# A decoder step on Trainium2: gathering the first expert's tokens channel-major from rounded high and low parts

## What is computed

```python
def moe_swiglu(h, w_router, b_router, we_gate, we_up, we_down):
    logits = (h @ w_router).astype(jnp.float32) + b_router.astype(jnp.float32)
    top_val, top_idx = lax.top_k(logits, TOP_K)          # TOP_K = 2 of 8
    gates = jax.nn.softmax(top_val, axis=-1)
    combine = jnp.sum(jax.nn.one_hot(top_idx, N_EXPERTS, dtype=jnp.float32) * gates[..., None], axis=-2)
    out = jnp.zeros_like(h)
    for e in range(N_EXPERTS):
        out = out + combine[..., e:e + 1] * swiglu(h, we_gate[e], we_up[e], we_down[e])
    return out
```

## Time and profile before

| | |
|---|---|
| median of three runs | 1937.91 us |
| profiled execution | 1939.48 us |
| its span | 1937.6 us |
| PE busy | 1819.5 us, 94% of the span |
| PE weight loads | 1424.8 us, 74% |
| DVE busy | 1270.0 us, 66% |
| ACT busy | 1065.4 us, 55% |
| POOL busy | 174.6 us, 9% |
| HBM read / written | 480.46 / 17.35 MB |

### The profile page before, as it was taken

One profiled execution on the slowest core, in us unless ns is written; L12 is line 12 of the kernel. 1 busy time (PEld: TensorE's weight loads), 2 busy tenths in 40 slices (PEclk: granted clock), 3 DMA queues, 4 the chain that ended last, 5 costly groups with the idle time before them and its releaser, 6 DMA issues.

```text
span 1937.6 us, 23755 instructions
## 1 busy us (share of the span) xinstructions
PE 1819.5 (94%) x8733; PEld 1424.8 (74%) x8733; DVE 1270.0 (66%) x1223; ACT 1065.4 (55%) x1054; POOL 174.6 (9%) x169
## 2 busy tenths in 40 slices
PE   7988988999998977988799999999999999999997
PEld 6776444899997955435488888888888888888884
DVE  5543133534436874123499898988889988889895
ACT  5433123332315357313387778778787787877672
POOL 4220010000002940010100000000000000000010
PEclk9989999999998988999799999999999999999999
DMA  9451316544435532416399999999999999999993
GB/s 308 157 160 56 120 66 227 181 145 134 147 123 180 196 126 83 138 52 201 134 378 384 368 391 366 386 381 366 392 368 391 379 374 390 364 397 369 385 384 132
DMA packets 236754, 497.88 MB, mean 257 GB/s; under 512 B 15010, under 2 KB 46899, under 8 KB 236670
## 3 DMA queue, kind: packets, MB, share of 16 engines
q1 hardware_dynamic: 223645, 479.11, 68.6%
q0 software_dynamic: 4544, 13.57, 1.9%
q10 hardware_dynamic: 8496, 4.33, 0.8%
HBM read 480.46 MB, written 17.35 MB: 257 GB/s over the span
## 4 chain that ended last, share of the span: by engine, by line
PE 53%; DMA 2%; DVE 2%; ACT 1%; issue 0%; POOL 0%; DVEq 0%; SPq 0%; ACTq 0%; POOLq 0%
PE bank L1150 45%; PE bank L547 4%; DMA big<-in_we_down 1%; PE bank L1209 1%; DMA small_ring<-in_we_down 1%; PE bank L1170 1%; PE bank L1122 0%; DVE big_r L2966 0%; PE bank L1160 0%; PE bank L1187 0%; PE bank L642 0%; ACT big_r L1728 0%; ACT small_ring_r L1728 0%; PE bank L913 0%; PE bank L934 0%
## 5 line engine op out<-in xcount | busy, mean ns | idle before, releaser
L1728 ACT ACTIVATE big_r<-small_ring 128x2048 fp32r<-128x2048 f32 x240 | 456.6, 1916 | 141.8 <-DMA small_ring<-in_we_up 49.0
L2966 DVE TENSOR_TENSOR small_ring_r<-small_ring,big_r 128x2048 fp32r<-128x2048 f32 x192 | 437.2, 2288 | 38.0 <-ACT big_r L1728 37.1
L1150 PE MATMUL bank<-big_r,hT_r 128*128 128x512 f32 x1024 | 384.1, 393 | 1.6 <-DVE kM_r L2972 1.6
L1150 PE MATMUL bank<-small_ring_r,hT_r 128*128 128x512 f32 x768 | 301.0, 392 | 0.0
L1150 PE MATMUL bank<-big_r,kM_r 128*128 128x512 f32 x704 | 274.2, 390 | 0.0
L2966 DVE TENSOR_TENSOR big_r<-big,small_ring_r 128x2048 fp32r<-128x2048 f32 x96 | 219.4, 2290 | 35.6 <-ACT small_ring_r L1728 35.4
L1150 PEld LDWEIGHTS bank<-big_r,hT_r 128*128 128x128 f32 x1024 | 192.3, 188 | 41.2 <-issue 1.8
L1728 ACT ACTIVATE small_ring_r<-big 128x2048 fp32r<-128x2048 f32 x96 | 183.5, 1916 | 50.4 <-DMA big<-in_we_up 27.5
L1150 PEld LDWEIGHTS bank<-small_ring_r,hT_r 128*128 128x128 f32 x768 | 144.2, 188 | 29.8
L1150 PEld LDWEIGHTS bank<-big_r,kM_r 128*128 128x128 f32 x704 | 132.3, 188 | 26.6
L1728 ACT ACTIVATE big_r<-big 128x2048 fp32r<-128x2048 f32 x59 | 113.2, 1919 | 44.4 <-DMA big<-in_we_up 12.8
(11 more groups left out here) (400 smaller groups left out, 2898.2 us busy)
## 6 DMA issues: line engine op xcount, KB each, us to landing
small_ring<-in_we_gate SPq DMA_DIRECT2D x80, 1024.0 KB, 6.3
small_ring<-in_we_up SPq DMA_DIRECT2D x64, 1024.0 KB, 6.1
big<-in_we_down SPq DMA_DIRECT2D x64, 1024.0 KB, 6.2
big<-in_we_up SPq DMA_DIRECT2D x48, 1024.0 KB, 7.0
small_ring<-in_we_down SPq DMA_DIRECT2D x48, 1024.0 KB, 6.2
big<-in_we_gate SPq DMA_DIRECT2D x32, 1024.0 KB, 5.5
small_ring<-in_w_gate SPq DMA_DIRECT2D x11, 1024.0 KB, 5.4
small_ring<-in_w_up SPq DMA_DIRECT2D x11, 1024.0 KB, 7.9
```

The source lines that it names most:

```text
L1150: ins = mm(dst, x_hi_lo[xa][kk], wcols, start=(m < 2 or j == 0) and kk == 0 and (xa, wa) == (0, 0), stop=(m < 2 or j == STAGES - 1) and kk ...
L1728: return A(out, in_, ACT.Copy)
L2966: V.tensor_tensor(low[i % PRING], raw[i % PRING], high[i % PRING].bitcast(F32), ALU.subtract) \
```

## The change

Expert 0's rows are no longer gathered as rows and transposed. ACT rounds `h` to high parts `rows_hi` (three copies of up to 128 x 1024), behind the transposed copies of `h`. DVE writes the low parts `rows_lo`: two ahead of the wait for the logits, the third ahead of the wait for the ranks. The selection is written in fp32r (`first_P`). PE then multiplies parts of `h` as the stationary operand by the selection as the moving one, so that the result is channel-major: for each of 8 channel groups and 3 row tiles one product of 128 columns, 24 for the high parts into banks 7 and 6 and 24 for the low parts into banks 5 and 4. ACT copies the high banks to `moe_x[0]`, DVE the low banks to `moe_x[1]`. Step 2 and the transposes are gone. Rounds after the first (which this input doesn't reach) keep the old way.

```diff
+        first_P = hT_r[:, 1024:1408].rearrange("p (t c) -> p t c", t=3)
+        rows_hi = [qz_r[:, 0:D], qz_r[:, D:2 * D], rounded("vM")[:, :]]
+        rows_lo = [kN_r[:, 0:D], v_r[:, 0:D], Pr_r[:, :]]
...
-            def gather(n, r=None):
+            def gather_first():
+
+                pe.wait_ge(*at("x_hi", "rows", 2))
+                pe.wait_ge(moe_sel, 1)
+                for part, (rows, top, done) in enumerate(((rows_hi, 7, moe_picked), (rows_lo, 5, moe_gathered))):
+                    for half in range(2):
+                        for k in range(4):
+                            c0 = (4 * half + k) * P
+                            for t in range(TILES):
+                                ins = mm(bank[top - half][:, k * P:(k + 1) * P], rows[t][0:ROWS[t], c0:c0 + P],
+                                         first_P[0:ROWS[t], t, :], start=t == 0, stop=t == TILES - 1)
+                        ins.then_inc(done, 1)
+
+            def gather(r):
...
             def expert_round(r):
                 rr = None if type(r) is int else r
-                gather(r * NE, rr)
+                if rr is None:
+                    gather_first()
+                    pe.wait_ge(moe_xhi, 2)
+                else:
+                    gather(r)
...
             norm_squares(5)
             to_hT(5, range(TILES))
+            for t in range(TILES):
+                act.wait_ge(*at("h", 5, t))
+                copy(rows_hi[t][0:ROWS[t]], h[0:ROWS[t], t, :]).then_inc(*sets("x_hi", "rows", t))
             act.wait_ge(*at("choice", "gap"))
...
                 weights_hi(r * NE, 0)
-                rows_out(r)
-                tokens_hi(r * NE)
+                if type(r) is int:
+                    for half in range(2):
+                        act.wait_ge(moe_picked, half + 1)
+                        copy(moe_x[0][:, 4 * half:4 * half + 4, :],
+                             bank[7 - half][:, :].rearrange("p (k c) -> p k c", k=4)).then_inc(moe_xhi, 1)
+                else:
+                    rows_out(r)
+                    tokens_hi(r * NE)
...
+            def rows_low(t):
+                dve.wait_ge(*at("x_hi", "rows", t))
+                V.tensor_tensor(rows_lo[t][0:ROWS[t]], h[0:ROWS[t], t, :], rows_hi[t][0:ROWS[t]].bitcast(F32), ALU.subtract)
+
+            dve.wait_ge(*at("v_out", 1))
+            rows_low(0)
+            rows_low(1)
             b = take("rt")
...
             step(V.tensor_tensor(gates, lg, m8, ALU.add))
+            rows_low(2)
             b = take("rank")
...
-                tokens_lo(r * NE)
+                if type(r) is int:
+                    for half in range(2):
+                        dve.wait_ge(*primed(moe_gathered, half + 1))
+                        V.tensor_copy(moe_x[1][:, 4 * half:4 * half + 4, :],
+                                      bank[5 - half][:, :].rearrange("p (k c) -> p k c", k=4)).then_inc(moe_xT, 1)
+                else:
+                    tokens_lo(r * NE)
```

More of the change, by code:

```diff
@@ L1161, in scatter @@
                    moe_y[:, hf * HALF:(hf + 1) * HALF], start=True, stop=True).then_inc(done, 1)
-            def gather(n, r=None):
-                pe.wait_ge(moe_sel, 1 if r is None else r + 1)
-                if r is not None:
-                    pe.wait_ge(moe_addedE, r * 6)
+            def gather_first():
[10 more added lines that the diff above has]
+            def gather(r):
+                pe.wait_ge(moe_sel, r + 1)
+                pe.wait_ge(moe_addedE, r * 6)
                 for half in range(2):
@@ L1173, in gather @@
                 for half in range(2):
-                    pe.wait_ge(moe_rows_at_hand, (half + 1) if r is None else r * 2 + (half + 1))
+                    pe.wait_ge(moe_rows_at_hand, r * 2 + half - 1)
                     for k in range(4):
@@ L2914, in select_first @@
                     dve.wait_ge(*primed(moe_gathered, r * 2 * NE))
+                chosen = first_P if type(r) is int else moe_P
                 for t in range(TILES):
                     rows = ROWS[t]
-                    ins = V.tensor_scalar(moe_P[0:rows, t, :], C("iota")[0:rows], posr[0:rows, t, 0:1], None, ALU.is_equal)
+                    ins = V.tensor_scalar(chosen[0:rows, t, :], C("iota")[0:rows], posr[0:rows, t, 0:1], None, ALU.is_equal)
                 ins.then_inc(moe_sel, 1)
```

## The result

Over 20 executions of each, the kernel before has a median of 1935.2 us and the changed one 1941.05 us. The ratio is 1.0035, with a 95% interval of 1.0025 to 1.0045: 5 to 9 us slower. The forecast was 1939 us with a range of 1933.5 to 1944.5, which holds the time. But it was 1.1 us above the median known then (1937.9, three runs), and the measured difference is 5.9 us by the medians and 6.8 by the ratio, just past the 0.3% that was set as the bound. Two executions far off the rest, 2097 us of the kernel before and 3676 us of f2, are left out of the ratios.

A forecast was written before the change was run, and what follows sets the result against it. PE was taken to set the pace from expert 0's first product on. Products 0, wait behind the gather -1.9 and clock +2.1 gave +0.2 us (1938.1 beside the median); a +1.0 correction made 1939 us, range 1933.5 to 1944.5.

The forecast's parts named there:

- likeliest case: The forecast's main case for the whole kernel: its own range 1936 to 1943 us, chance 0.64.
- What bounds the kernel: Expert stage, some 960 us: PE sets the pace from expert 0's first product, so shifting its start shifts the end.
- The products of the gather: Gather on PE: 48 products at a weight-load floor of 0.215 take 10.3 us, old gather 10.4; term 0.
- Behind the gather: From gather's end to expert 0's first product: 2.9 us becomes 1.0, gain 1.9 us, bounds 1.6 and 2.2.
- The clock behind it: Expert 0's first products: clock stays low for about 4.5 us, costing 2.1 us, bounds 1.4 and 2.8.
- Hidden work: ACT's three roundings and DVE's three subtractions (1.1 us each) fit into waits for router, logits and ranks; cost 0.
- The first refill: First weight refill by DMA leaves after expert 0's first twelve products, at 966.1 against 966.03 before.
- The correction: Old gather sometimes regains its clock early, making the kernel before about 3 us faster; given a third, adds 1.0 us.
- Quick gather: Rival: the 48 gather products take 0.11 us each, total time about 1933 us; chance 0.13.
- Dear narrow products: Rival: 128 columns cost as much as 512 in the gather; about 1940, or 1946 to 1948 us; chance 0.11.
- Swallowed at the end: Rival: small early shifts vanish in the last expert, where PE waits 3.1 us for DVE; 1938 us; chance 0.12.

The follow-up runs named there:

- f2: e2 plus 24 narrow rounded products of 8 columns ahead of the gather, in place of f1's 12 wide ones; 1938.3 us, ratio to before 1.0014.
- e2: Changed kernel with the third row tile padded with zeros, so all 48 gather products have 128 rows; 1935.3 us, ratio to before 1.0001.
- e1: Changed kernel with its 48 products reordered so that four products of one row tile stand together; 1936.5 us, ratio to before 1.0003.
- f4: Changed kernel, row-count changes left in, plus f1's 12 wide products ahead of the gather; 1942.4 us, ratio to before 1.0039.
- e4: Changed kernel with all 48 products over 64 rows, so expert 0's result is not the reference's; one execution, 1936.7 us.
- g3: e1 (unpadded, products of a row tile together) plus f1's 12 wide products ahead of the gather; 1935.8 us, ratio to before 1.0010.
- f3: Kernel before plus 3 float32 products of 512 columns ahead of its old gather; 1935.4 us, ratio to before 0.9998.
- f1: e2 plus 12 wide rounded products of 512 columns, result unused, in PE's wait ahead of the gather; 1931.8 us, ratio to before 0.9978.
- e3: Kernel before plus only ACT's three high parts and DVE's three low parts, which nothing reads; 1935.2 us, ratio to before 1.0001.
- g1: f1 with 8 wide products in place of 12; 1932.7 us, ratio to before 0.9998.

## Why the prediction was right, and where it was wrong

That the time lies in the range is in part luck. The likeliest sum was -1.9 for the hops, +2.1 for the clock and 0 for the products, +0.2 in all, and +1.0 for the correction. The products cost 6.0 us more, and the clock's 2.1 did not reach the end. The difference came out at 5.9 where 1.1 was forecast. The time fell within 2 us of 1939 because the median of the kernel before, 1937.9 from three runs, came down to 1935.2 with twenty; from 1937.9 it would have been 1943.8, inside the range by 0.7 and above the likeliest case's own range of 1936 to 1943.

- **What bounds the kernel: right.** What the gather lost reached the end: 5.9 us on the gather, 5.8 us in the medians (changed kernel against e2). In all traces but e1 and f4, expert 0's first product lies 974.0 to 975.2 us ahead of the span's end, so a shift of it shifts the end.
- **The products of the gather, "this term is 0": wrong, and the step that failed.** It measured +6.0 us (16.38 against 10.38). The floor of 0.215 was right for a run of products with one row count: 10.49 and 10.48 us for 48 in e2 and e4 are 0.218 each. What is missing is a wait of 0.19 at each of 31 changes. The lesson stands in the trace of before, and I did not look there. The weight loads of its old gather, with the idle time before each in brackets:

```profile
951.53 0.34 PEld L1170 LDWEIGHTS bank<-h,hT 128*128 128x128 f32 x1 [0.52 <-issue]
953.37 0.50 PEld L1170 LDWEIGHTS bank<-h,hT 64*128 64x128 f32 x2 [1.50 <-issue]
955.37 0.50 PEld L1170 LDWEIGHTS bank<-h,hT 128*128 128x128 f32 x2 [1.50 <-issue]
956.39 0.34 PEld L1170 LDWEIGHTS bank<-h,hT 128*128 128x128 f32 x1 [0.52 <-issue]
```

  A load waits 0.52 us behind one of the same row count and 1.50 behind one of another. At three changes in a gather of twelve long records this costs little; at 31 in 48 short ones it is a third of the time.
- **Behind the gather, gain 1.9: right.** 2.92 us became 0.94, so 2.0.
- **The clock behind it, loss 2.1: right at its place, but "nothing hides it" was wrong.** It stayed at 0.50 for 5 us of expert 0, and 72 products took 2.3 us more. From expert 0's first product to the end of the span, though, the changed kernel took 974.0 us, the kernel before 974.6. The same holds for the other traces: 974.1, 974.7 and 974.2 in e2, f2 and g3, whose first 72 products took 19.0 to 19.5 us, and 974.4 and 974.8 in f3 and f1, where they ran at full clock. That it does not come back in the gather held. The Trainium skill says in "TensorE: Matmul & The Clock Gate", section "What's actually happening", that activity releases the throttle. This trace does not bear that out for PE's busy time taken by itself: the 48 products kept PE busy for 16 us without a gap, and the granted clock stayed at 0.50.
- **Hidden work, cost 0: right** (e3), though DVE's subtractions took 1.22 each, not 1.1.
- **The first refill, 966.1: late.** It left at 969.49, since it follows expert 0's first twelve products, which began 3.2 us later than forecast.
- **The correction, +1.0: right in direction, perhaps too small.** 7.63 us for the same old gather in e3, 2.8 less than in the execution first shown. From the gather's start to the first product that kernel took 13.3 us in the one trace and 10.6 in the other; e2 took 11.4, between the two, and the medians of e2 and of the kernel before are level. The working had a slip: of the 10.4 us, 1.3 were at full clock already, so a return after 4 us saves 2.5 and not 3.2. How often the clock comes back early was not counted; level medians would fit with more often than the third that I gave it, but the intervals are too wide to tell.
- **The rivals.** Quick gather: out in the changed kernel, real once the clock is back (f1). Dear narrow products: 0.34 us is just over the 0.33 at which I let it decide, and the time fell between its two (about 1940, and 1946 to 1948), but its reason is false. Swallowed at the end: in part. I counted the records of the experts' line from its first: the 3528th of 4032 starts 831.3 us later in the kernel before, 831.9 in the changed one and in e2, 831.0 in f1 and 832.7 in f2. The 4000th starts at 949.0, 948.5, 948.4, 948.5 and 949.0. So in these traces what a cold start of expert 0 costs is given back, while a later first product is not. The differences of 2 to 3 us behind the first 72 products are 0.5 to 1.7 at the 3528th and about 0.5 or less at the 4000th, so a large part goes in the last expert. Of the rest, f1 loses 1.1 in its wait near 979, and the kernel before loses 1.5 between the 504th and the 2000th product in this execution, without a cause that I know. In the kernel before, the chain through the last expert goes through three loads of `w_down` that took 9.3 to 10.7 us to land. Which wait takes the difference up was not tried.

In sum, up to expert 0's first product: +6.0 for the products and -2.0 behind them, 4.0 us against the execution first shown; against the old gather with its clock back early, as in e3, 17.3 - 10.6 = 6.8 us. The clock behind the gather adds little or nothing at the end. The measured 5.9 by the medians, and 6.8 by the ratio (0.35% of 1935.2), lie between these two or at the upper one.

## What to carry to other kernels

When short products with few columns are strung together, look at the row count of neighbours: order them by it, or pad the odd tile with zeros so that it never changes. Before a stretch of narrow products, find the granted clock in the windows; if PE waits there anyway at the low clock, wide products in that wait can buy it back, as 12 of them did here (f1); look in the trace whether it is kept. A price that is right at its place need not reach the end: compare the stretch from there to the end of the span as well. And take the price of a new shape from rows with the same pattern of shapes, not only from rows with the same shape.

## What the runs showed of the hardware that I had not expected

- In these traces a weight load did not run beside a product with another row count (128 against 64). Each change cost 0.19 us at 1.2 GHz: 48 products took 16.4 us with 31 changes, 11.6 us with 7, and 10.5 us with none, for 64 rows as for 128. At 2.4 GHz a change cost 0.14 us (f4, g3): a mixed triple took 0.62 us, three products without a change 0.33.
- The same 48 narrow products that leave the clock at 0.50 when they start there (e2, 10.5 us) kept it at 1.00 when they started there (f1 and g1, 5.3 us); in g1 it was lost right behind them. With 31 changes of row count among them it was lost inside the gather (f4), with 7 right behind it (g3). These are single executions.
- A start of expert 0 at the low clock cost 2.3 to 2.9 us over its first 72 products and, in single executions, nothing that shows from its first product to the end of the span (974.0 to 974.7 us cold, 974.4 to 974.8 warm).
